# Six feed-forwards and a differential attention that are fed the residual without its norm factor

## The reference, cut to what matters

```
h += attention_ab(rms(h))      h += square(relu(rms(h) @ w1)) @ w2       # mlp0
h += attention_mla(rms(h))     h += square(relu(rms(h) @ w1)) @ w2       # mlp1
h  = rms(h)                                                           # final norm of block 1
h += 0.5 * swiglu(rms(h))                                             # swi0
h += diff_attention(rms(h))    h += 0.5 * swiglu(rms(h))                 # da, swi1
h += 0.5 * swiglu(rms(h))      h += retention(rms(h))                    # swi2, rt
h += 0.5 * swiglu(rms(h))                                             # swi3
```

## Time and profile before

| what | value |
|---|---|
| median of 3 runs | 1803.74 us (1799.4 to 1803.89) |
| the profiled execution: its own time | 1801.26 us |
| its span in the trace | 1799.5 us |
| TensorE matmul busy | 1733.1 us (96%) |
| VectorE / ScalarE busy | 968.4 us (54%) / 799.4 us (44%) |
| mean granted TensorE clock | 0.986 |

### The profile page before, as it was taken

One profiled execution on the slowest core, in us unless ns is written; L12 is line 12 of the kernel. 1 busy time (PEld: TensorE's weight loads), 2 busy tenths in 40 slices (PEclk: granted clock), 3 DMA queues, 4 the chain that ended last, 5 costly groups with the idle time before them and its releaser, 6 DMA issues.

```text
span 1799.5 us, 27978 instructions
## 1 busy us (share of the span) xinstructions
PE 1733.1 (96%) x11639; PEld 1558.5 (87%) x11654; DVE 968.4 (54%) x1051; ACT 799.4 (44%) x944; POOL 25.3 (1%) x47
## 2 busy tenths in 40 slices
PE   7989999979999989999999999999999999999999
PEld 6846999875799979999897999989998999879998
DVE  5565555566555555454676554454446444554544
ACT  4245444456444444433576434354435444334342
POOL 1000000010000000000010000000000000000000
PEclk8989999999999999999999999999999999999999
DMA  9302555430355545545434455545454554235550
GB/s 370 142 1 82 211 186 186 164 129 24 121 199 186 188 151 192 189 170 192 153 119 174 176 187 187 187 164 188 176 189 173 187 186 164 94 116 189 185 188 24
DMA packets 41719, 291.88 MB, mean 162 GB/s; under 512 B 4720, under 2 KB 4864, under 8 KB 7472
## 3 DMA queue, kind: packets, MB, share of 16 engines
q1 hardware_dynamic: 38880, 281.04, 43.5%
q0 software_dynamic: 2224, 8.55, 1.4%
q10 hardware_dynamic: 544, 1.26, 0.2%
HBM read 289.76 MB, written 1.06 MB: 162 GB/s over the span
## 4 chain that ended last, share of the span: by engine, by line
PE 86%; DVE 7%; ACT 5%; issue 2%; DMA 1%; SPq 0%; DVEq 0%; ACTq 0%
PE up L199 16%; PE up L201 15%; PE up L200 15%; PE accs L199 10%; PE accs L200 10%; PE accs L201 10%; PE accs L584 1%; DVE wlo L193 1%; ACT whi L189 1%; PE up L301 1%; DVE xn L358 1%; PE up L563 1%; DVE h L414 1%; PE up L1633 1%; ACT xn L308 1%
## 5 line engine op out<-in xcount | busy, mean ns | idle before, releaser
L193 DVE TENSOR_TENSOR wlo<-raw,whi 128x2048 fp32r<-128x2048 f32 x266 | 610.6, 2298 | 455.9 <-ACT whi L189 455.9
L189 ACT CAST whi<-raw 128x2048 fp32r<-128x2048 f32 x266 | 505.3, 1903 | 223.2 <-PE accs L201 155.3
L199 PE MATMUL up<-xh,whi 128*128 128x256 f32 x2112 | 599.3, 284 | 0.0
L201 PE MATMUL up<-xh,wlo 128*128 128x256 f32 x2112 | 597.6, 283 | 0.0
L200 PE MATMUL up<-xl,whi 128*128 128x256 f32 x2112 | 597.6, 283 | 0.0
L199 PEld LDWEIGHTS up<-xh,whi 128*128 128x128 f32 x2112 | 405.1, 192 | 4.0 <-issue 1.0
L200 PEld LDWEIGHTS up<-xl,whi 128*128 128x128 f32 x2112 | 405.1, 192 | 3.1 <-issue 0.5
L201 PEld LDWEIGHTS up<-xh,wlo 128*128 128x128 f32 x2112 | 405.1, 192 | 0.0
L199 PE MATMUL accs<-whi,hidh 128*128 128x512 f32 x632 | 248.2, 393 | 0.3
L200 PE MATMUL accs<-wlo,hidh 128*128 128x512 f32 x632 | 246.7, 390 | 0.0
L201 PE MATMUL accs<-whi,hidl 128*128 128x512 f32 x632 | 246.0, 389 | 0.0
(11 more groups left out here) (233 smaller groups left out, 1631.0 us busy)
## 6 DMA issues: line engine op xcount, KB each, us to landing
raw<-weights SPq DMA_DIRECT2D x266, 1024.0 KB, 4.8
gain<-gains POOLq DMA_DIRECT2D x10, 512.0 KB, 4.0
h<-x_in SPq DMA_DIRECT2D x2, 512.0 KB, 5.7
tabs<-consts POOLq DMA_DIRECT2D x1, 1024.0 KB, 7.8
out<-h SPq DMA_DIRECT2D x2, 512.0 KB, 2.6
tabs<-consts ACTq DMA_DIRECT2D x1, 768.0 KB, 13.8
hid<-rel_scratch POOLq DMA_DIRECT2D x1, 768.0 KB, 6.9
hidh<-rel_scratch POOLq DMA_DIRECT2D x1, 768.0 KB, 8.2
```

The costliest lines, as they stand in the source:

```text
L189: nc.scalar.copy(whi[:, m % SPLIT, :], raw[:, m % RAW, :]).then_inc(hi_ready, 1)
L193: nc.vector.tensor_tensor(wlo[:, m % SPLIT, :], raw[:, m % RAW, :], whi[:, m % SPLIT, :].bitcast(F32), ALU.subtract).then_inc(lo_ready, 1)
L199: nc.tensor.matmul(out_ap, sh, mh, start=first, stop=False)
L201: return nc.tensor.matmul(out_ap, sl, mh, start=False, stop=last)
```

## The change

Seven handoffs (`RAW_Q` = q 1, 3, 4, 5, 6, 7, 9) no longer wait for the norm. `gain_piece` forms `xn = h * gain`, and this is projected. The sums of squares are still made, but beside the work; the token's factor is applied later:

- mlp: relu and square of a scaled value is the square of the scale, so `add_piece` multiplies the output by `1 / (mean + eps)` per token.
- swiglu: the a half is multiplied by the factor before silu. `spread_rows` brings the factor into the layout of the hidden values (TensorE, then a VectorE copy into `row_scale`). The b half gets its factor in `add_piece`, with the 0.5.
- differential attention: v is copied with the factor; for q and k the norm's eps is scaled instead (`eps_raw`).

The transposes of block 1 are issued in halves (`turn_part`), one half ahead of the last out slab's last piece. `stay_warm` goes from these handoffs, but for q = 4. The first slab (`first_wide`) begins with k chunks 0 to 3 for both output blocks.

Every other in slab of the feed-forwards uses `project_wide`: `xh` and `xl` lie in one tensor `xhl`, and one matmul of 512 columns takes both against `whi`. The two results lie side by side in a bank, one bank for each output block, and are added afterwards: ScalarE copies the one half, VectorE adds the other. `zero_sums` goes.

```diff
+        def project_wide(n, banks, blocks=(0, 1)):
+            for j in blocks:
+                bank = banks[j]
+                for k in range(KC):
+                    if k:
+                        nc.tensor.matmul(bank[:, 0:T], W(wlo, n, k, j * P, (j + 1) * P), xh[:, k, :],
+                                         start=False, stop=False)
+                    mm = nc.tensor.matmul(bank, W(whi, n, k, j * P, (j + 1) * P), xhl[:, :, k, :],
+                                          start=k == 0, stop=k == KC - 1)
...
@@ last_slabs
             if q is not None and q != FINAL_Q:
                 turn_block(pe, q, 0)
+            if q in RAW_Q and q != FINAL_Q:
+                turn_part(pe, q, 2)
             project_out(n + 1, *f1, last=True, blocks=(1,), halves=(1,)).then_inc(slab_used, 1)
-            if q is not None:
+            if q is not None and q not in RAW_Q:
                 stay_warm(WARM)
             if q == FINAL_Q:
                 turn_block(pe, q, 0)
                 stay_warm(WARM)
+                turn_part(pe, q, 2)
...
+        def first_wide(pe, n, q):
+            def part(first, low):
...
+            pe.wait_ge(lo_ready, n + 1)
+            pe.wait_ge(xl_ready, 4 * q + 2)
+            pe.wait_ge(xh_ready, 4 * q + 3)
+            part(0, False)
+            turn_part(pe, q, 3)
+            pe.wait_ge(xl_ready, 4 * q + 3)
+            part(0, True)
+            pe.wait_ge(xh_ready, 4 * q + 4)
+            part(4, False)
+            pe.wait_ge(xl_ready, 4 * q + 4)
+            part(4, True).then_inc(slab_used, 1)
+            pe.wait_ge(lo_ready, n + 2)
+            project_wide(n + 1, in_banks(1)).then_inc(slab_used, 1)
...
+        def raw_scalar(act, q, s, n):
...
+                square_piece(act, s, 0)
+                square_piece(act, s, 1)
+            take_high(act, q, (0, 1, 2))
+            split_high(act, n + 1)
+            take_high(act, q, (3,))
...
+            square_piece(act, s, 2)
...
+        def raw_vector(dve, q, s, n, u, factor):
+            split_low(dve, n)
+            add_piece(dve, u, 0, n, factor)
...
+            gain_piece(dve, q, s, 0)
+            add_piece(dve, u, 1, n, factor)
...
+                gain_piece(dve, q, s, 1)
+                take_low(dve, q, (0, 1))
+                add_piece(dve, u, 2, n, factor)
+                gain_piece(dve, q, s, 2)
+                take_low(dve, q, (2,))
+            take_low(dve, q, (3,))
+            split_low(dve, n + 1)
+            raw_stats(dve, s)
...
@@ feed_scalar, feed_vector (swiglu)
+            elif j == 0:
+                act.wait_ge(slab_used, after(n + 1, i, RAW))
+                nc.scalar.copy(flat2(slot), sum_parts(0)[0 if begin else 1]).then_inc(S("feed_side"), 1)
+            else:
+                act.wait_ge(S("feed_sum"), after(SUMS[name] + 3 * g + 2, i, 3 * per))
+                nc.scalar.activation(slot, slot, ACT.Silu).then_inc(S("feed_act"), 1)
+                act.wait_ge(slab_used, after(n + 1, i, RAW))
+                nc.scalar.copy(flat2(side), sum_parts(1)[1]).then_inc(S("feed_side"), 1)
...
+                    nc.vector.tensor_tensor(flat2(part), sum_parts(second)[0], flat2(part), ALU.add
+                                            ).then_inc(S("feed_sum"), 1)
...
@@ da_scalar
-                nc.scalar.copy(vd[:, p % 2, :, :].rearrange("p t n -> p (t n)"), da_bank(s)).then_inc(S("d_v"), 1)
+                act.wait_ge(rstd_ready, ROOTS[6] + 1)
+                for t in range(TB):
+                    ins = nc.scalar.activation(vd[:, p % 2, t, :], da_bank(s)[:, t * T:(t + 1) * T], ACT.Copy,
+                                               scale=rstd[:, t:t + 1])
```

More of the change, by code:

```diff
@@ L73 @@
 SLABS = _n
+PLAIN_NORMS = (0, 2, 4, 9)
+ROOT_NORMS = (5, 6, 7, 8, 10)
+STATS = {}
+ROOTS = {}
+_n = 0
+_m = 0
+for _s in range(11):
+    STATS[_s] = _n
+    ROOTS[_s] = _m
+    _n += 1 if _s in PLAIN_NORMS else 3
+    _m += 2 if _s in PLAIN_NORMS else 1 if _s in ROOT_NORMS else 0
 FED = {}
@@ L79 @@
         _n += MLP_G if _name[:3] == "mlp" else SWI_G
+SUMS = {}
+SIDES = {}
+ACTED = {}
+_n = 0
+_k = 0
+_m = 0
+for _name, _count in STAGES:
+    if _name[:3] in ("mlp", "swi"):
+        SUMS[_name] = _n
+        SIDES[_name] = _k
+        ACTED[_name] = _m
+        _n += MLP_G if _name[:3] == "mlp" else 3 * SWI_G
+        _k += MLP_G if _name[:3] == "mlp" else 2 * SWI_G
+        _m += 0 if _name[:3] == "mlp" else SWI_G
 C_ID, C_ONES, C_BLK, C_ROTA, C_ROTC, C_FLIP = (k * P for k in range(6))
@@ L210, in project_features @@
             return mm
+        def project_wide(n, banks, blocks=(0, 1)):
[7 more added lines that the diff above has]
+                                          start=k == 0, stop=k == KC - 1)
+                    if k == 0:
+                        nc.tensor.matmul(bank[:, 0:T], W(wlo, n, k, j * P, (j + 1) * P), xh[:, k, :],
+                                         start=False, stop=False)
+            return mm
         def project_tokens(n, bank, lo=0, hi=IN_W, blocks=range(TB)):
@@ L318, in root_block, with take_high @@
                                  scale=1.0 / D).then_inc(std_ready, 1)
[L320 to L321 removed]
+        def take_high(act, q, parts):
+            for b in parts:
+                t = b // 2
                 act.wait_ge(turned, 4 * q + b + 1)
@@ L431, in spread @@
             return mm
-        def zero_sums():
-            for b in range(4):
-                nc.tensor.matmul(accs[:, b, :], zero[:, 0:P], zero[:, :], start=True, stop=False)
+        sub_rstd = sb("sub_rstd", [P, 2 * T])[:, :]
+        side = sub_rstd
+        sub_o = sb("sub_o", [P, 2 * T])[:, :]
+        row_scale = sub_o[:, 0:T]
+        FEED_NORM = {"mlp0": 1, "mlp1": 3, "swi0": 5, "swi1": 7, "swi2": 8, "swi3": 10}
+        ROWS = {"swi0": 0, "swi1": 1, "swi2": 2, "swi3": 3 + RT_HEADS}
         def feed(name, kind):
@@ L467, in run_feed_tensor @@
             order, ins, per = feed(name, kind)
-            first_slabs(pe, FIRST[name], q)
-            zero_sums()
+            first_wide(pe, FIRST[name], q)
+            if kind != "mlp":
+                spread_rows(pe, name)
             turns = (len(order) - 4) // RAW
-            with pe.Fori(0, turns) as i:
+            for s in order[2:2 + RAW]:
+                feed_tensor(pe, name, kind, s, None, per)
+            with pe.Fori(1, turns) as i:
                 for s in order[2:2 + RAW]:
@@ L488, in feed_tensor @@
             if what == "in":
-                if g >= 1 and j == 0:
-                    pe.wait_ge(S("feed_hidden"), after(FED[name] + g - 1, i, per))
-                bank = up[g % per] if kind == "mlp" else up[2 * (g % per) + j]
-                project_features(n, bank).then_inc(slab_used, 1)
+                if kind == "mlp":
+                    pe.wait_ge(S("feed_sum"), after(SUMS[name] + g, i, per))
+                    project_wide(n, in_banks(0)).then_inc(slab_used, 1)
+                else:
+                    pe.wait_ge(S("feed_sum"), after(SUMS[name] + 3 * g - 2 + 2 * j, i, 3 * per))
+                    project_wide(n, in_banks(j)).then_inc(slab_used, 1)
             else:
                 pe.wait_ge(S("feed_hidden_low"), after(FED[name] + g + 1, i, per))
-                project_out(n, lambda k: hidh[:, g % per, k, :], lambda k: hidl[:, g % per, k, :]
-                            ).then_inc(slab_used, 1)
+                project_out(n, lambda k: hidh[:, g % per, k, :], lambda k: hidl[:, g % per, k, :],
+                            first=g == 0 and i is None).then_inc(slab_used, 1)
         def ahead(n, name, kind, left):
@@ L523, in feed_vector, with whole @@
                 split_low(dve, n + 2, i)
-            if what == "out" or j != (kind != "mlp"):
+            if what == "out":
                 return
-            dve.wait_ge(S("feed_act"), after(FED[name] + g + 1, i, per))
+            slot = hid[:, g % per, :]
+            begin = n == FIRST[name]
+            if begin and kind != "mlp":
+                raw_root(dve, FEED_NORM[name])
+            def whole(part, second):
+                if begin:
+                    dve.sem_inc(S("feed_sum"), 1)
+                else:
+                    nc.vector.tensor_tensor(flat2(part), sum_parts(second)[0], flat2(part), ALU.add
+                                            ).then_inc(S("feed_sum"), 1)
```

314 lines of the change are left out of this document (212 added, 102 removed).

## The result

| kernel | median us | lowest, highest | ratio to before, 95% interval |
|---|---|---|---|
| before | 1803.76 | 1799.4, 1803.89 | |
| changed | 1757.76 | 1755.78, 1758.75 | 0.9752 [0.974, 0.9765] |

What follows compares the result with a forecast made beforehand. TensorE was taken as the bound: busy 96% of the span, 86% of the last-ending chain. Terms -21.7, +3.0, -27.1, -3.4 and +1.0 sum to -48.2, taking 1801.26 to 1753.1 us; range 1740 to 1771.

Steps and rivals of the forecast that it cites:

- Wide in slabs: 114 feed-forward in slabs: one 512-column matmul replacing two of 256 saves 0.012 us a pair, 0.19 a slab; -21.7 us.
- Feed-forward ends: At all six ends TensorE waits about 0.8 us for the last hidden values, lengthened by added passes; +3.0 us.
- Handoffs: Seven handoffs no longer wait for the norm, TensorE's own work setting most of their length; -27.1 us in sum.
- TensorE alone has to do 13.4 us: Handoffs: TensorE's own work from block 0's end to the first slab's end takes 13.4 us, against 17.55 at q = 1.
- q = 4: Handoff into swi0, where two norms follow each other: the second goes off the path; -5.7 us, 2.1 from the clock.
- I take full clock: At q = 4: TensorE stands still 2.4 us at most, so no half clock; 2.1 us of the gain.
- q = 5: Handoff into differential attention: the second slab's `wlo` still ends last, but earlier; -2.35 us.
- `zero_sums` and `spread_rows`: Feed-forwards: dropping `zero_sums` six times gives -5.3 us, adding `spread_rows` four times costs +1.9; -3.4 us together.
- The rest: Attention stages: extra v-copy and root instructions cost differential attention +1.0 us (0 to 2.4); no change counted for the others.
- the wide matmul gives little: Rival, 12%: in wide slabs the second 256-column piece pays most of the fixed 12 ns again; 1770 to 1775 us.
- VectorE or the clock holds the handoff: Rival, 15%: at handoffs `wlo` comes 1.5 us late (1763 us), or the clock falls without the zeros (1766).
- Slower by `feed_sum`: Rival, 4%: in feed-forwards TensorE waits for additions that free a bank pair; 1823 us at 1 us a group.

Runs made afterwards that it cites:

- e9_da_plain: e8_all with the plain norm back for differential attention (q = 5) and without the zeros ahead of its values; 1754.51 us.
- e1_three: Changed kernel with each 512-column matmul of `project_wide` as two of 256 columns; 1776.95 us.
- e8_all: Changed kernel with zero matmuls at two idle differential-attention places, half an out-slab block ahead of the `hidl` wait, 20 instead of 12 zeros into swi0; 1750.69 us.
- e10_more: e8_all with zero matmuls in three more idle places, two in latent attention and one in retention; 1749.83 us.

## Why the prediction was right, and where its sum was off

- **Wide in slabs** (-21.7): right in mechanism, about a tenth too large. Taking it out costs 19.2 by the medians and some 20 by the stages, 0.17 to 0.18 us a slab for the 0.19.
- **Feed-forward ends** (+3.0): the wait is there at all six ends, 0.9 us. Removing it gives nothing at q = 2 and q = 8, where I had 0.7 and 1.4, and 1.4 at the kernel's end, where I had 0.9. The 0.5 and 0.6 at q = 5 and q = 7 stand in the handoffs of my sum.
- **Handoffs** (-27.1): "TensorE alone has to do 13.4 us" holds; at q = 1 the first slab ends 12.9 us behind the start of add 0, with TensorE alone in the chain. The parts by experiment: leaving the zeros out 2.6 us in each, the order of the first slab 1.7. Together that is 4.3 of the 4.6 us that q = 1 gained. The norm put back in these handoffs, with its wait, was run for q = 5 only (e9_da_plain); for the others its place off the path is read from the chain. The handoffs behind attentions and swi1 (five with q = 1) take 13.0 us, 0.4 less than counted. That makes up for the wide slabs' shortfall, so part of the feed-forwards' agreement to 0.1 us is luck.
- **q = 4** (-5.7): this holds where the clock holds (swi0's segment -9.09 for -9.4). "I take full clock" was one execution's answer: four of nine profiles with 12 zeros have 6.8 us at 1.2 GHz there, and the second profile of the changed kernel loses 2.6 us to it.
- **q = 5**: `wlo` of the second slab still ends last, as said, but it hangs on TensorE's last transposes through the rounding and the rest of `xhl`, which is why zeros ahead of them cost their full time there. The chain, and TensorE's timeline at its release:

```profile
845.99 0.45 PE ups L389 x4
...
846.46 0.59 ACT xhl L418
...
847.08 0.69 DVE xhl L520
847.77 2.20 DVE wlo L223
...
850.02 0.39 PE L229 MATMUL accs<-whi,xhl 128*128 128x256 f32 x1 [1.23 <-DVE wlo L223]
```

From the add to this release it is 14.5 us; before it was 18.1. So the handoff gained 3.5 of the 3.75 counted, and the stage itself gave back 1.3 instead of 1.0.

- **`zero_sums` and `spread_rows`** (-3.4): not tried by themselves; each feed-forward's segment comes out within 0.35 us of its sum, but these terms could hide behind others that miss the other way.
- **The rest** (differential attention +1.0, the other attentions nothing): the step that failed. It took every stretch outside the handoffs to run at the clock that it had in the trace of before. In the first profile the attentions are the whole miss: 3.6 us in the differential attention, 1.2 and 1.0 in the others. Of the 3.6, 3.1 go with the two stretches at 1.2 GHz; 0.5 remain where the clock holds (123.15 against the 122.64 of the sum).
- **Rivals**: "the wide matmul gives little" is refuted by e1_three. "VectorE or the clock holds the handoff" is half right: VectorE nowhere beyond the waits counted at q = 4 and 5, the clock at q = 4 in some executions; its larger share was in stages that the change hardly touches. "Slower by `feed_sum`" did not happen: the page's chain has TensorE at 88%, and swi1 to swi3 come out 0.2 us from the sum.

Still open: why an idle time of the same 1.6 us is followed by 1.2 GHz in one execution and not in another, reached half a microsecond earlier or later. The runs show that it does, and that none of the filled places in the differential and the latent attention had a stretch in the profiles taken; they do not show what decides.

The best version is e8_all or e10_more, which differ by less than their spreads: 1750.69 and 1749.83, some 7 to 8 us below the changed kernel.

## What to carry to other kernels

Where an edit shortens everything ahead of a stage, compare the later stages by their own length as well, and look at the granted clock before looking for a cause in the code: an untouched stage can lose a microsecond or three. A profile shows one draw of the half-clock stretches; profile the same kernel twice before building a story on one of them. Matmuls on zeros pay only where TensorE would stand idle anyway: in idle places of 1.6 us and more they gave 1.1 to 1.5 us for each stretch of 3.4 us that was gone, in the retention, where a second idle place stayed open, they gave nothing, and in handoffs without idle time twelve of them cost 2.5 to 2.6.

## What the runs showed of the hardware

- One kernel's half-clock stretches differ between executions: two in the differential attention and none at q = 4 in one profile; one there, and 6.8 us at q = 4, in the next. The same instructions of the differential attention took 126.25, 124.70 and, shifted by zeros ahead of them, 123.14 us.
- A moving operand of two pieces 8 KB apart shows no cost here: the 512-column matmul over `xhl` stands 0.23 to 0.24 from the next, like the contiguous ones of the out slabs, and a wide slab takes 5.59 us against the 5.56 added up from contiguous ones.
- Fixed time belongs to the matmul (with its weight load) and not to its columns, also where 256 and 512 columns come in turn: 19.2 us for 114 x 16 matmuls saved is 10.5 ns each, and the 20 us by stages 11 ns, near the 12 ns that the earlier trace rows gave. The Trainium skill (TensorE: Matmul & The Clock Gate, "Back-to-back issue gap") gives 2.5 ns for an isolated matmul; in this stream, with a weight load for each, the measurement is four times that. The section itself says that in such a stream the weight loads set the spacing too.
